# Three fp32r passes in place of fp32 products for the first mixer's input projections

## The reference, cut to what matters

```
mod = c_act @ w_mod + b_mod;  shift, scale, gate = split(mod, 3)
h = rmsnorm(x, g_pre) * (1.0 + scale) + shift
proj = h @ w_in
(mu, mv, mi, mf, mz, aq, ak, av, az, sq, sk, sv, sz) = split(proj)
y_m = mlstm_branch(mu, mv, mi, mf, ...) * silu(mz)      # recurrent branch, 4 heads of 96
y_a = swa_branch(aq, ak, av, a_sinks) * silu(az)        # sliding window, 6 heads of 64
y_s = stickbreak_branch(sq, sk, sv) * silu(sz)          # 4 heads of 64
y = concat([y_m, y_a, y_s]) @ w_out
x = x + gate * rmsnorm(y, g_post)

mlstm_branch: cu = silu(causal_conv(u, conv_w, conv_b)); q = cu @ wq; k = cu @ wk (per head);
    then a scan over the sequence: s = (q k^T) * exp(dmat - m), num = w_inter * (C q) + s v, ...
    C = carry * C + sum(ws * v k); h = num / max(|den|, exp(-m)), normalized per head
```

## Time and profile before

| | us |
|---|---|
| median of 3 runs | 3527.76 (3524.14 to 3536.26) |
| profiled execution: its own time | 3528.56 |
| profiled execution: span | 3526.5 |
| last weight tile of `w_mod` taken by DVE | 76.4 |
| barrier "loaded" to first product of the attention | 91.4 to 552.9 |
| mean granted TensorE clock, share of full speed | 0.943 |

### The profile page before, as it was taken

The page is one execution under the profiler, slowest core; times in us unless marked ns, Lnnn a source line. Parts: engine busy times, 40 slices in busy tenths (PEclk is TensorE's granted clock), DMA queues, the critical chain, the costliest instruction groups (busy, mean ns, idle before and its releaser), DMA issues.

```text
span 3526.5 us, 37209 instructions
## 1 busy us (share of the span) xinstructions
PE 3287.0 (93%) x15471; PEld 2432.9 (69%) x15471; DVE 1530.8 (43%) x2264; ACT 687.6 (19%) x1151; POOL 75.1 (2%) x148
## 2 busy tenths in 40 slices
PE   3998999999699899889999999989989899999997
PEld 2455445465455688767888888877867788888886
DVE  5235003462411555634434334358984534334334
ACT  1232103451201455532000000012133100000002
POOL 1000000010000400000000000000000000000000
PEclk6999999889689899989999999999989999999998
DMA  6100110001110000021111111101100211111111
GB/s 230 69 18 12 36 39 9 30 1 72 61 48 27 7 1 1 1 90 60 48 48 48 48 48 48 48 18 48 36 20 24 71 49 48 48 48 48 48 36 48
DMA packets 127077, 153.21 MB, mean 43 GB/s; under 512 B 18503, under 2 KB 114667, under 8 KB 125419
## 3 DMA queue, kind: packets, MB, share of 16 engines
q1 hardware_dynamic: 126379, 134.72, 12.1%
q10 hardware_dynamic: 576, 16.78, 1.1%
HBM read 138.90 MB, written 12.58 MB: 43 GB/s over the span
## 4 chain that ended last, share of the span: by engine, by line
PE 53%; DVE 2%; ACT 1%; DMA 0%; issue 0%; DVEq 0%; SPq 0%; ACTq 0%
PE ps L1135 41%; PE ps L1112 9%; PE ps L1208 1%; PE ps L707 0%; DVE sc L2123 0%; PE ps L1245 0%; DVE h_low L2127 0%; DVE sc L1687 0%; DMA out_dram<-sc 0%; PE ps L723 0%; DVE ht L1729 0%; ACT big L1625 0%; ACT h_high L1643 0%; ACT sc L1646 0%; DVE h_low L2255 0%
## 5 line engine op out<-in xcount | busy, mean ns | idle before, releaser
L1135 PE MATMUL ps<-h_high,w_high 128*128 128x512 f32 x1408 | 550.8, 391 | 15.0 <-DVE h_low L2127 15.0
L1135 PE MATMUL ps<-h_high,w_low 128*128 128x512 f32 x1408 | 550.2, 391 | 0.0
L1135 PE MATMUL ps<-h_low,w_high 128*128 128x512 f32 x1408 | 550.0, 391 | 0.0
L680 PE MATMUL ps<-ht,ring 128*128 128x512 f32 (+1 forms) x768 | 340.5, 603 | 6.6 <-ACT ht L1301 2.8
L1112 PE MATMUL ps<-h_high,ring_parts 128*128 128x512 f32 x1024 | 322.2, 397 | 22.5 <-DVE h_low L2127 9.0
L1135 PEld LDWEIGHTS ps<-h_high,w_high 128*128 128x128 f32 x1408 | 265.8, 189 | 70.6 <-issue 15.4
L1135 PEld LDWEIGHTS ps<-h_high,w_low 128*128 128x128 f32 x1408 | 265.8, 189 | 55.2
L1135 PEld LDWEIGHTS ps<-h_low,w_high 128*128 128x128 f32 x1408 | 265.7, 189 | 55.3
L1588 ACT ACTIVATE sc<-ps 128x1024 f32<-128x1024 f32 x44 | 45.3, 1029 | 1237.0 <-PE ps L1135 1237.0
L680 PEld LDWEIGHTS ps<-ht,ring 128*128 128x128 f32 (+1 forms) x768 | 143.5, 189 | 198.3 <-issue 189.1
L2103 DVE TENSOR_TENSOR xt<-ps,xt 128x1024 f32<-128x1024 f32 x176 | 211.6, 1221 | 147.0 <-PE ps L1135 147.0
(11 more groups left out here) (320 smaller groups left out, 4033.4 us busy)
## 6 DMA issues: line engine op xcount, KB each, us to landing
ring<-in_ffn_w_gate_dram SPq DMA_DIRECT2D x22, 1024.0 KB, 5.3
ring<-in_ffn_w_up_dram SPq DMA_DIRECT2D x22, 1024.0 KB, 5.3
ring<-in_ffn_w_down_dram SPq DMA_DIRECT2D x22, 1024.0 KB, 4.8
ring<-in_w_mod_dram SPq DMA_DIRECT2D x8, 1536.0 KB, 7.6
ring<-in_conv_w_pw_dram SPq DMA_DIRECT2D x24, 512.0 KB, 3.9
x_kept<-xt ACTq DMA_DIRECT2D x2, 4096.0 KB, 11.1
xt<-x_kept ACTq DMA_DIRECT2D x2, 4096.0 KB, 12.9
ring<-in_w_in_dram SPq DMA_DIRECT2D x3, 1536.0 KB, 6.7
```

The lines of the kernel that those rows point to most:

```text
L680: last = mm(o[0:m, 512 * half:512 * half + 512], w(k), src(k)[:, 512 * half:512 * half + 512], start=k == 0, stop=k == kk - 1)
L1135: return mm(o, w, rows, start=start and part_ == 0, stop=stop and part_ == 2)
```

## The change

- `h` is held as two fp32r tiles `hin` (high and low), and every input-projection weight tile is split in high and low: `high` on ACT, `low` on DVE. `split_chunk`, `split_tokens` and `filled` make three fp32r products for each fp32 one. All 464 products of the input projections go this way (336 of 512 columns, 64 of 392, 64 of 384). The ring tiles get narrower (96 or 128 columns each, 21 tiles in place of 9) and are freed by the split, not by `used`.
- `root(0)` and `spread(0)` come ahead of the `w_mod` tiles, and DVE multiplies x by the root (`xr`) between those tiles. After the barrier DVE applies gain and shift by one `tensor_scalar`, ACT copies the high part, DVE subtracts.
- The `T_MVG` and `T_AV` weights get buffers of their own outside the ring.
- Queries and keys are made per block of 128 tokens in the scan (`queries_keys`), one block ahead. The decay rows (`selr` products), the mask and the exponentials of all eight blocks come ahead of the scan.
- Fills: 16 ahead of the scan, 8 in each of its blocks (5 before), and outputs 2 to 9 all go through bank 7 (`elif 3 <= f <= 9` in `filled`), one after the other's copy. With every second output `fill_copies` on ACT splits off the high part of a coming tile (`if n % 2`).
- Several memsets of the gate chain stand behind `gates_up` now, and `low(T_MU + 3)` stands in that chain.

```diff
-                if n:
-                    spread(n)
+                spread(n)
...
-            spread(0)
...
+            root(0)
             for k in range(KC):
+                tt(xr[:, k, :], xt[:, k, :], bank(6, 2), mul)
                 v.wait_ge(w_ready[k % 2], arrives[k])
...
-            root(0)
             stage(v, "loaded")
-            scaled(xt, 40, ht, misc, s.h_mul)
+            low(T_MU, KC * M_D)
+            for k in range(KC + 1):
+                if k < KC:
+                    ts(xr[:, k, :], xr[:, k, :], misc[:, 40 + k:41 + k], misc[:, 16 + k:17 + k], mul, add).then_inc(s.h_mul, 1)
+                if k >= 1:
+                    v.wait_ge(s.h_hi, k)
+                    tt(hin[1][:, k - 1, :], xr[:, k - 1, :], hin[0][:, k - 1, :].bitcast(F32), sub).then_inc(s.h_ok, 1)
+            v.wait_ge(s.big_hi, 1)
+            tt(mvg[1], mvg_raw, mvg[0].bitcast(F32), sub).then_inc(s.big_split, 1)
+            low(T_MU + 1, KC * M_D)
...
+            def high(t, n=KC * P):
+                a.wait_ge(w_ready[t % 2], arrives[t])
+                f(parts_of(t)[0][:, 0:n], raw_of(t)[:, 0:n], ACT.Copy).then_inc(s.w_hi, 1)
+            high(T_MU, KC * M_D)
             for k in range(KC):
                 a.wait_ge(s.h_mul, k + 1)
-                f(ht[:, k, :], ht[:, k, :], ACT.Identity, bias=misc[:, 16 + k:17 + k]).then_inc(s.h_ok, 1)
+                f(hin[0][:, k, :], xr[:, k, :], ACT.Copy).then_inc(s.h_hi, 1)
+            a.wait_ge(s.mvg_in, 16)
+            f(mvg[0], mvg_raw, ACT.Copy).then_inc(s.big_hi, 1)
...
+            def split_chunk(j_, t, m, norm=None, between=None):
+                pe.wait_ge(s.w_split, splits(t))
...
+                    for p_, (wp_, rp_) in enumerate(PASSES):
+                        last = mm(o[0:m, 512 * half:512 * half + 512], w(wp_, k), hin[rp_][:, k, 512 * half:512 * half + 512],
+                                  start=k == 0 and p_ == 0, stop=k == KC - 1 and p_ == 2)
...
+            low(T_MU + 2, KC * M_D)
+            convolved(0)
+            v.wait_ge(s.gates_up, 1)
             v.memset(hr(4), 1.0)
             chain(v.memset(sc[:, 0, :], 0.0))
...
             v.wait_ge(s.rows_b, 1)
+            low(T_MU + 3, KC * M_D)
...
             copy_out(J_IN + 5, [cp(mu[:, 1, 3:S + 3], m=M_D)])
+            high(T_MU + 3, KC * M_D)
             a.wait_ge(s.rows_c, 1)
...
+            fill(4)
             for t in range(TB):
                 if t >= 2:
-                    pe.wait_ge(s.ktok_copied, t - 1)
+                    pe.wait_ge(s.md_done, t - 1)
...
+                last.then_inc(s.d_done, 1)
                 fill(1)
+            queries_keys(0)
+            fill(4)
+            pe.wait_ge(s.md_done, TB)
             for t in range(TB):
+                if t + 1 < TB:
+                    queries_keys(t + 1)
+                pe.wait_ge(s.qk_copied, 2 * t + 2)
...
+                fill(4)
                 if t >= 1:
                     pe.wait_ge(s.mstate, t)
...
+                fill(FILLED(t) - fills[0])
                 pe.wait_ge(s.ms_weighted, t + 1)
...
+            def queries_keys(t):
...
+                for w in range(2):
+                    for h in range(M_H):
+                        last = mm(ps[0:M_D, 512 + 512 * w + P * h:512 + 512 * w + P * h + P], qk[:, w, h, :],
+                                  cu[:, h, P * t:P * t + P], start=True, stop=True)
...
+                f(mq[:, t % 2, :], ps[0:M_D, 512:1024], ACT.Copy, scale=M_D ** -0.5).then_inc(s.qk_copied, 1)
+                f(mkt(t), ps[0:M_D, 1024:1536], ACT.Copy).then_inc(s.qk_copied, 1)
...
+                    elif 3 <= f <= 9:
+                        pe.wait_ge(s.fill_free, f)
+                    elif f == 10:
+                        pe.wait_ge(s.mstate, TB)
...
+                    if n % 2:
+                        t = T_MZ + n // 2 + 2
+                        high(t, KC * (M_D if t < T_AZ else P))
...
                 v.wait_ge(s.mexp_done, t + 1)
+                tt(weigh[:, t], by_heads(0), weigh[:, t], mul).then_inc(s.ms_weighted, 1)
+                fill_lows(FILLED(t))
                 v.wait_ge(s.mo_done, t + 1)
```

More of the change, by code:

```diff
@@ L320, in build @@
         T_IN = len(tiles)
-        T_MVG, T_MU, T_MZ, T_AZ, T_SZ, T_AQ, T_AK, T_SQ, T_AV = range(T_IN, T_IN + 9)
-        tiles += [1, 1, 1, 1, 1, 6, 2, 1, 2]
+        T_MU, T_MZ, T_AZ, T_SZ, T_AQ, T_AK, T_SK, T_SQ = (T_IN + n for n in (0, 4, 8, 11, 13, 16, 17, 19))
+        tiles += [1] * 13 + [2] * 3 + [1] * 5
         T_YM = len(tiles)
@@ L777, in rows_turned, with split_of @@
                 last.then_inc(s.rowcols, 1)
+            def split_of(t, width):
+                hi, lo = (w[:, 0:KC * width].rearrange("p (k n) -> p k n", k=KC) for w in parts_of(t))
+                return lambda p_, k: (hi, lo)[p_][:, k, :]
+            def split_chunk(j_, t, m, norm=None, between=None):
+                pe.wait_ge(s.w_split, splits(t))
+                w, o = split_of(t, m), group(j_)
+                order = [(half, k) for half in range(2) for k in range(KC)]
+                if norm is not None:
+                    order = [(half, k) for k in range(KC) for half in range(2)]
+                for half, k in order:
+                    if norm is not None and half == 0:
+                        pe.wait_ge(s.h_ok, H_OK[norm] + k + 1)
+                    if between is not None and half and k == 0:
+                        between()
+                    for p_, (wp_, rp_) in enumerate(PASSES):
+                        last = mm(o[0:m, 512 * half:512 * half + 512], w(wp_, k), hin[rp_][:, k, 512 * half:512 * half + 512],
+                                  start=k == 0 and p_ == 0, stop=k == KC - 1 and p_ == 2)
+                last.then_inc(s.g_out, 1)
@@ new lines, in split_tokens @@
+            def split_tokens(j_, pair, n, count):
+                pe.wait_ge(s.big_split, count)
+                hi, lo = (w.rearrange("p (k n) -> p k n", k=KC) for w in pair)
+                for i in range(TB // 2):
+                    o = group(j_ + i)
+                    for b in range(2):
+                        for k in range(KC):
+                            for p_, (wp_, rp_) in enumerate(PASSES):
+                                last = mm(o[:, 512 * b:512 * b + n], hin[rp_][:, k, P * (2 * i + b):P * (2 * i + b) + P],
+                                          (hi, lo)[wp_][:, k, :], start=k == 0 and p_ == 0, stop=k == KC - 1 and p_ == 2)
+                    last.then_inc(s.g_out, 1)
@@ L787, in filled @@
                         pe.wait_ge(s.fill_free, f - 1)
[L788 to L791, removed]
+                w = split_of(t, m)
+                for p_, (wp_, rp_) in enumerate(PASSES):
+                    last = mm(bank(o)[0:m, :], w(wp_, k), hin[rp_][:, k, 512 * (f % 2):512 * (f % 2) + 512],
+                              start=k == 0 and p_ == 0, stop=k == KC - 1 and p_ == 2)
@@ L842, in _ @@
+                pe.wait_ge(s.ktok_copied, t + 1)
+                for h in range(M_H):
+                    mm(ps[:, 2048 + 97 * h:2048 + 97 * h + 97], mq[:, t % 2, P * h:P * h + P], ct[:, h, :],
                        start=True, stop=True)
                 for h in range(M_H):
[L844 to L847, removed]
@@ L872, in _ @@
                 last.then_inc(s.ht_done, 1)
-                if n:
-                    fill(2)
+                fill(2)
             fill(8 * FILLS - fills[0])
[L877 to L881, removed]
+            pe.wait_ge(s.mstate, TB)
+            for i in range(3):
+                split_chunk(J_ATT + i, T_AQ + i, P)
+            split_tokens(J_ATT + 3, av_part, A_W, 2)
+            for i in range(5):
+                split_chunk(J_ATT + 7 + i, T_AK + i, P)
             stage(pe, "attention_in")
@@ L1770, in _ @@
             convolved(1)
-            convolved(2)
+            low(T_MZ, KC * M_D)
             v.wait_ge(s.rowcols, 1)
@@ L1824, in _ @@
                 tt(mz[:, h, c_], tmp, mz[:, h, c_], mul)
+            fill_lows(8 * FILLS)
+            v.wait_ge(s.big_hi, 2)
+            tt(av_part[1], av_raw, av_part[0].bitcast(F32), sub).then_inc(s.big_split, 1)
+            for i in range(6):
+                low(T_AQ + 2 + i)
             stage(v, "attention_in")
```

324 lines of the change are left out of this document (186 added, 138 removed).

## The result

| | before | after |
|---|---|---|
| median, us | 3527.86 | 3499.04 |
| lowest to highest that agree, us | 3519.92 to 3536.26 | 3477.71 to 3513.14 |
| ratio, 95% interval | | 0.9907 (0.9887 to 0.9927) |
| span of the profiled execution | 3526.5 | 3500.8 |
| first product of the attention | 552.86 | 507.98 |

The kernel is faster by 0.9%, 29 us, where 54 were forecast; 3499 lies above the range of 3460 to 3495. The times do not spread evenly: of 15 runs six lie between 3477.7 and 3481.2 and nine between 3497.2 and 3513.1, with nothing between, and the mean clock goes with them (0.938 or 0.939 against 0.930 to 0.933). The profiled execution (3502.56) belongs to the upper ones. The runs of before show no such gap. One run of before, at 6645.9, stands apart from all others and is left out of the second row.

What follows compares the result with a forecast made beforehand. PE, busy 93% of the span, was taken as the bound. PE work -76.9, loading and h +13.9, gate chain +5.9, scan +6.9, after scan -6.5, clock +3: -53.7 from 3528.6, so 3474.9 (median 3474), range 3460 to 3495.

Steps and rivals of the forecast that it cites:

- The products: Input projections on PE: three fp32r products replace each fp32 one, saving 59.5 us at 512 columns and 16.1 at narrower widths.
- the rival that narrow ones do not shrink: Products of 392 and 384 columns stay at 0.2276 per instruction: 20 us less saved, 3494; chance 0.10.
- Queries and keys: Made per block of 128 columns at 0.126 us per instruction: 16.2 us for 13.8, a loss of 2.4.
- Loading and h: From weight loads through the barrier to the tokens: later first slot and bare splits, +13.9 us together.
- the sum: All terms up to the attention's start: -53.7 us, from 3528.6 to 3474.9, carried unchanged to the end.
- the short rows of the loads: Loads in rows of 384 or 256 bytes, under the 512 for full rate: charged nothing.
- The gate chain: From gates_up to rows_d: 27.8 us in place of 22.8, PE idle 5.9 before the turned rows.
- Scan and its end: Decay rows and scan +6.9 us, with blocks of 11.8 and 4.0 idle; heads after it -6.5, with 5.4 idle.
- The rival of slow handovers: Scan blocks bound by handovers between engines, 8 us of waiting each: +10, 3538, slower than before; chance 0.03.
- The clock: PE's clock falls once more, at the longest new idle time (5.9 us): +3 us, bounds 0 and 9.
- waits add up: Slow loads, slow tensor_scalar (4), clock falls at four gaps (6), scan handovers (5): 15 us more, 3489; chance 0.17.

Runs made afterwards that it cites:

- the experiments with the root: Two idle products at the attention barrier, root inverted after the first two w_mod tiles, against the kernel with only those idle products: median 3474.85 us, ratio 0.9847.
- the early splits: First mu tile and values' weights split before the barrier, against the changed kernel plus two idle products at the attention barrier: median 3474.19 us, ratio 0.9845.
- the repair: Gate chain on DVE shortened (memsets earlier, last mu low part later), against the changed kernel plus two idle products at the attention barrier: median 3475.97 us, ratio 0.9857.
- warm handover: Changed kernel plus two idle fp32 products of 448 columns between the last projection and the attention barrier: median 3481.79 us, ratio 0.9879.

## Why the prediction was wrong

**The products: right.** 0.18 per fp32r instruction of 392 columns (0.177 forecast), so the rival that narrow ones do not shrink falls. One group of 1024 tokens takes 506.87 - 495.99 = 10.88 us (from one group's end, where ACT copies it out, to the next), 0.680 per product against 0.683. Queries and keys cost nothing extra (0.109, not 0.126 each): 2 us better.

**Loading and h: right** to 1 us; the experiments with the root and the early splits took back part of what the sum had charged. Nothing charged for the short rows of the loads was right too: PE waited for no DMA.

**The gate chain: right**, 5.6 idle for 5.9, and 1.6 for 1.7 after the repair.

**Scan and its end: right.** 11.50 a block for 11.8, 3.9 for 4.0, 3.6 idle at the heads for 5.4. The rival of slow handovers falls: no block waits.

**The clock: this step failed.** It read "I take one more, at the longest (5.9): +3 (bounds 0 and 9)". In the profiled execution PE was busy at the lower level for 3.4 us after 121, 8.4 of the 10 from 190 to 200, 23 from 214 to 238, 3.4 from 332 to 336 and 3.4 from 345 to 355: half of the 41.6, 21, is lost, where the fall before cost 3. That is 18 more than before where the sum has 3 more, 15 too many; the smaller waits and the quicker queries took 5 to 6 back, and the attention starts 8.8 later than 499.2.

Two errors are in it. First, the four falls behind waits cost 9, which is 6 more than before and inside the bounds of that term; the fall from 214 costs the other 11.5 and stood in no term and in no bound. I looked only for idle times, and this one needs none: the wait of 1.1 ahead of it could go and the fall stayed. It comes among thin products (decay rows four partitions high, 128 columns) with single fills between them, which lie in one stretch ahead of the scan. Feeding that stretch with full-height fp32 products ended the fall. Second, I carried the difference at the attention's start "through to the end", while the clock fell there in 13 of 21 runs, for 19 us.

The misses add up: the profiled execution is 3502.56 - 3474.9 = 27.7 above the sum, about 8.8 of it up to the attention and 19 behind it. The forecast 3474 is near the runs without the fall at the attention (3478 to 3481), in part by luck: there too the fall among the decay rows was missed and the smaller waits made up for some of it. The median is one with the fall at the attention. Of the rivals, "waits add up" put falls at all four gaps 6 above the sum's 3; behind waits they cost 6 more than before, between the two. Its other terms did not come: no load made PE wait, the `tensor_scalar` took 0.81, and no block of the scan waited.

The Trainium skill (TensorE: Matmul & The Clock Gate, HAM oscillation — how this bites in real kernels) warns that waits between short stretches of work make the clock fall again and again. The falls at 121 and 190 agree in that each came behind a wait (3.1 and 5.6 us), though the work between those two was long; the one from 214 had only 1.1 us of waiting ahead of it and came without that too.

**What stays open.** Why the clock falls at the attention in some executions of one kernel and not in others, and what in the 30 us before it tips it. Filling the idle time is enough, fp32 in place of fp32r just ahead is enough, and neither was shown to be necessary. What in the thin stretch lets the clock go (the height, the short products, or fp32r in the fills) was not separated, since the products put in differ from what was there in height, in form and by being added work. Whether moving the decay rows back into the scan would do as well as the idle products was not tried.

## What to carry to other kernels

When a change replaces slow products by quicker ones, PE's idle times and thin stretches weigh more: price each not by its length alone but also by what the clock at half costs in the work behind it, and look at the granted clock of every stretch of the profile after, those that were not edited too. One profiled execution can hide that a kernel has two groups of times; take the list of all runs. A few idle products are cheap beside a fall: two of them at a barrier were worth 17 us of the median, eight among thin rows 8 to 10. And compare a fall of the clock by its length, not by the granted clock of a fixed stretch: the same 24 us gave 0.51 and 0.62 from 214 to 238, since one began 5 us earlier.

## What the hardware showed that I had not expected

- The clock stayed at half for 44 us of unbroken PE work at the start of the attention (0.52 from 509 to 555), and then came back in the same work.
- PE can be busy for 24 us on end and have the lower level for that long, with DMA at rest (warm handover: busy for 24.00 from 214 to 238, DMA share 0.00, the lower level from 208.5 to 232), in a stretch of products of 4 and 96 partitions with single fp32r fills between them; with one full-height fp32 product of 448 columns more in each step it got 1.00.
- fp32r instructions of 512 columns with 96 output features follow each other a little more slowly than with 128: 0.695 us per product (30 of them from 164.26 to 185.11 after) against 0.680.
